# A hybrid encoder layer: small vectors moved ahead of two x tiles, constant rows written by ScalarE, one weight load given its own place

## The reference

```python
h = rms_norm(x, attn_norm)
q, k, v, f_logit, u, cv, cb, cc, g = split(h @ w_in)      # 512,512,512,8,512,512,512,512,3*1024
y_a = forgetting_attention(q, k, v, f_logit, b_f) @ w_proj_attn   # logit bias F[t]-F[s], F = cumsum(log_sigmoid(f))
y_b = multiscale_pool(u, pool_w, pool_scale) @ w_proj_pool        # trailing means of 2/4/8/16 tokens
y_c = short_gated_conv(cv, cb, cc, conv_w) @ w_proj_conv          # B * conv3(C * v)
gates = sigmoid(g + b_gate)
x = x + (gates0 * y_a + gates1 * y_b + gates2 * y_c) @ w_out
a, b = split(rms_norm(x, ffn_norm) @ w_gate_up)           # 2 * 2816
x = x + (silu(a) * b) @ w_down
out = rms_norm(x, final_norm)
```

## Time and profile before

| what | value |
|---|---|
| median of 3 runs | 783.92 us (782.99 to 784.42) |
| profiled execution, its own time | 783.68 us |
| its span (first to last instruction) | 781.2 us |
| TensorE busy | 769.5 us (98%) |
| VectorE busy | 633.4 us (81%) |
| ScalarE busy | 410.1 us (52%) |
| GpSimd busy | 22.8 us (3%), 47 instructions |
| mean granted TensorE clock | 0.998 |
| HBM traffic | 82.87 MB read, 4.19 MB written |

### The profile page before, as it was taken

How to read it: one execution, slowest core, us unless ns; L and a number is a source line. 1 busy time by engine, 2 the same in 40 slices (tenths; PEclk the granted TensorE clock), 3 DMA queues, 4 the chain that set the end, 5 groups by cost and what they waited for, 6 DMA issues and landing times.

```text
span 781.2 us, 12728 instructions
## 1 busy us (share of the span) xinstructions
PE 769.5 (98%) x4491; PEld 682.0 (87%) x4491; DVE 633.4 (81%) x1001; ACT 410.1 (52%) x695; POOL 22.8 (3%) x47
## 2 busy tenths in 40 slices
PE   7999999999999999999999999999999999999996
PEld 5888888888889999999988888999999998888885
DVE  6888686868698878776744599899999986799997
ACT  7265564556445545455434554555555552655554
POOL 5011010100000000000000000000000000000001
PEclk9999999999999999999999999999999999999999
DMA  7433232223243434333363422433333355353422
GB/s 226 118 81 91 69 84 62 77 74 81 81 108 82 108 103 114 93 98 109 108 230 94 152 93 81 122 102 103 109 109 108 110 174 175 117 180 132 149 85 107
DMA packets 130438, 87.81 MB, mean 112 GB/s; under 512 B 5628, under 2 KB 118324, under 8 KB 130388
## 3 DMA queue, kind: packets, MB, share of 16 engines
q1 hardware_dynamic: 129876, 87.08, 37.8%
q0 software_dynamic: 512, 0.07, 0.1%
HBM read 82.87 MB, written 4.19 MB: 111 GB/s over the span
## 4 chain that ended last, share of the span: by engine, by line
PE 96%; DVE 1%; DMA 1%; issue 1%; ACT 0%; POOL 0%; SPq 0%; POOLq 0%; ACTq 0%
PE bank L791 11%; PE bank L795 11%; PE bank L793 11%; PE bank L1170 6%; PE bank L1168 6%; PE bank L1166 6%; PE bank L1222 4%; PE bank L1221 4%; PE bank L981 4%; PE bank L979 4%; PE bank L977 4%; PE bank L1220 4%; PE bank L1015 2%; PE bank L1016 2%; PE bank L1017 2%; PE bank L1059 2%
## 5 line engine op out<-in xcount | busy, mean ns | idle before, releaser
L791 PE MATMUL bank<-operands,whi 128*128 128x512 f32 x384 | 151.6, 395 | 1.3 <-DVE operands L1862 1.3
L795 PE MATMUL bank<-operands,wlo 128*128 128x512 f32 x384 | 149.7, 390 | 0.0
L793 PE MATMUL bank<-operands,whi 128*128 128x512 f32 x384 | 149.6, 389 | 0.0
L1853 DVE TENSOR_TENSOR wlo<-raw,whi 128x1024 fp32r<-128x1024 f32 x55 | 67.1, 1222 | 37.5 <-ACT whi L1286 36.8
L791 PEld LDWEIGHTS bank<-operands,whi 128*128 128x128 f32 x384 | 72.1, 188 | 17.1 <-DVE operands L1862 1.9
L795 PEld LDWEIGHTS bank<-operands,wlo 128*128 128x128 f32 x384 | 72.1, 188 | 15.4
L793 PEld LDWEIGHTS bank<-operands,whi 128*128 128x128 f32 x384 | 72.1, 188 | 14.6 <-issue 0.2
L1286 ACT CAST whi<-raw 128x1024 fp32r<-128x1024 f32 x55 | 57.5, 1049 | 31.1 <-PE bank L1063 21.0
L1166 PE MATMUL bank<-sums_hi,whi 128*128 128x256 f32 x240 | 67.9, 283 | 0.0
L1170 PE MATMUL bank<-sums_hi,wlo 128*128 128x256 f32 x240 | 67.9, 283 | 0.0
L1168 PE MATMUL bank<-sums_lo,whi 128*128 128x256 f32 x240 | 67.9, 283 | 0.0
(11 more groups left out here) (294 smaller groups left out, 1950.7 us busy)
## 6 DMA issues: line engine op xcount, KB each, us to landing
raw<-in_w_in_dram SPq DMA_DIRECT2D x105, 256.0 KB, 3.2
raw<-in_w_gate_up_dram SPq DMA_DIRECT2D x88, 256.0 KB, 3.3
raw<-in_w_down_dram SPq DMA_DIRECT2D x55, 256.0 KB, 2.9
big_x<-in_x_dram SPq DMA_DIRECT2D x8, 512.0 KB, 6.5
raw<-in_w_out_dram SPq DMA_DIRECT2D x16, 256.0 KB, 3.3
raw<-in_w_proj_attn_dram SPq DMA_DIRECT2D x8, 256.0 KB, 4.1
raw<-in_w_proj_pool_dram SPq DMA_DIRECT2D x8, 256.0 KB, 4.0
raw<-in_w_proj_conv_dram SPq DMA_DIRECT2D x8, 256.0 KB, 4.2
```

The costliest lines, as they stand in the source:

```text
L791: nc.tensor.matmul(banks[b][:, 0:width], whi[:, s, w], op(hi + k * S), start=a, stop=False)
L793: nc.tensor.matmul(banks[b][:, 0:width], whi[:, s, w], op(lo + k * S), start=False, stop=False)
L795: mm = nc.tensor.matmul(banks[b][:, 0:width], wlo[:, s, w], op(hi + k * S), start=False, stop=z)
L1853: nc.vector.tensor_tensor(wlo[:, s, :], raw[:, s, :], whi[:, s, :].bitcast(F32), ALU.subtract).then_inc(w_lo, 1)
```

## The change

Three edits, independent of each other.

1. SyncE issues the six small transfers after the second tile of x, and the third and fourth tile after them. The first weights stay where they were, behind all of these.
2. The constant rows: GpSimd adds pairs of neighbouring columns of the identity matrix to get four columns of 128 (`stat` columns 40 to 43), turns two of them negative, and does so before the first `root`. ScalarE then writes each 512-column region as ones times such a column, four activations between `diff_hi(0)` and the cast of the forget columns. The twelve GpSimd instructions are gone.
3. The seventh pair of w_down blocks (`SPARE` = 6) lands in the free columns 7168 to 8191 of `early_32` instead of slot 0 of `raw`, and is issued when `used` reaches NU. The tenth pair (9) then needs slot 0 only to be free of the fourth pair (3).

```diff
-            for t in range(TB):
-                load_x(t)
+            load_x(0)
+            load_x(1)
             for src, at in ((attn_norm, V_ATTN), (ffn_norm, V_FFN), (b_gate, V_GATE),
                             (pool_scale, V_SCALE)):
...
+            for t in range(2, TB):
+                load_x(t)
...
             for r in range(R):
-                sp.wait_ge(w_lo, NU - SLOTS + r + 1 if r < SLOTS else NU + 2 * (r - SLOTS) + 2)
+                if r == SPARE:
+                    sp.wait_ge(used, NU)
+                elif r == SPARE + SLOTS:
+                    sp.wait_ge(w_lo, NU + 2 * (SPARE - SLOTS) + 2)
+                else:
+                    sp.wait_ge(w_lo, NU - SLOTS + r + 1 if r < SLOTS else NU + 2 * (r - SLOTS) + 2)
...
+            pool.wait_ge(consts, 4)
+            for n, (a, row) in enumerate(F_ROWS):
+                r = (1 - a) * HD + row
+                nc.gpsimd.tensor_tensor(stat[:, F_COLS + n:F_COLS + n + 1], ident[:, r:r + 1],
+                                        ident[:, r + 1:r + 2], ALU.add).then_inc(f_consts, 1)
+            pool.wait_ge(f_consts, 4)
+            nc.gpsimd.tensor_scalar(stat[:, F_COLS:F_COLS + 2], stat[:, F_COLS:F_COLS + 2], -1.0,
+                                    None, ALU.mult).then_inc(f_consts, 1)
+
             for t in range(TB):
                 root(t, x1_var, x1_rstd)
 
-            begun = 0
-            for tiles, first, fill in ((Q2, 0, -1.0), (K2, 2, 1.0)):
-                for a in range(2):
-                    rows = op(tiles[a])
-                    nc.gpsimd.memset(rows.bitcast(F32), 0.0).then_inc(f_consts, 1)
...
-            pool.wait_ge(f_consts, F_CONSTS)
+            pool.wait_ge(f_rows, 4)
...
             diff_hi(0)
-            act.wait_ge(f_consts, F_CONSTS)
+            act.wait_ge(f_consts, 5)
+            for n, at in enumerate(Q2 + K2):
+                nc.scalar.activation(op(at), ones[:], ACT.Copy,
+                                     scale=stat[:, F_COLS + n:F_COLS + n + 1]).then_inc(f_rows, 1)
+            act.wait_ge(f_rows, 4)
...
+        def down_raw(k, half, n=1):
+            if k == SPARE:
+                return early_32[:, SPARE_AT + half * HALF:SPARE_AT + (half + n) * HALF]
+            return raw[:, k % SLOTS, half * HALF:(half + n) * HALF]
```

More of the change, by code:

```diff
@@ L398, in hybrid_block @@
         fe = work[0:H, PAD + 3 * S:PAD + 4 * S]
-        F_LOW, F_CONSTS = 32, 12
+        F_LOW, F_COLS, F_ROWS = 32, 40, ((0, 0), (1, 0), (0, 2), (1, 2))
         vec_rows = work[0:N_VECS, PAD + 5 * S:PAD + 5 * S + P]
@@ L415, in hybrid_block @@
         AB, DB_, FB_, EB = (2, 3), (6, 7), (4, 5), (0, 1)
-        N1 = 0
+        SPARE, SPARE_AT = 2 * SLOTS, 2 * DB * S - D
         ROWS4 = [(r,) for r in range(4)] + [(r, r + 1) for r in range(4, R - 1, 2)] + [(R - 1,)]
@@ L445, in hybrid_block @@
         f_in = sem("f_in")
-        f_consts = sem("f_consts")
+        f_consts, f_rows = sem("f_consts"), sem("f_rows")
         final_g_in = sem("final_g_in")
         landed = [sem(f"landed{s}") for s in range(SLOTS)]
+        spare_in = sem("spare_in")
         loads_begun = sem("loads_begun")
@@ L483, in landed_down @@
         def landed_down(k):
+            if k == SPARE:
+                return spare_in, 32
             before = (NU - PARTS + LOADS - PER_TURN * len(TURNS) + TURN_LOADS) // SLOTS * 32
             for q in range(k % SLOTS, k + 1, SLOTS):
-                before += 16 if q == 2 * R else 32
-            return k % SLOTS, before
+                before += {SPARE: 0, 2 * R: 16}.get(q, 32)
+            return landed[k % SLOTS], before
         def wait_full(eng, b, stage, i, k):
@@ L666, in load_down @@
             def load_down(k, blocks):
-                s = k % SLOTS
+                signal = spare_in if k == SPARE else landed[k % SLOTS]
                 for at, (row, c) in enumerate(blocks):
-                    sp.dma_start(raw[:, s, at * HALF:(at + 1) * HALF],
+                    sp.dma_start(down_raw(k, at),
                                  w_down[row * P:(row + 1) * P, c * HALF:(c + 1) * HALF]
-                                 ).then_inc(landed[s], 16)
+                                 ).then_inc(signal, 16)
             for r in range(R):
-                sp.wait_ge(w_lo, NU - SLOTS + r + 1 if r < SLOTS else NU + 2 * (r - SLOTS) + 2)
+                if r == SPARE:
[4 more added lines that the diff above has]
+                    sp.wait_ge(w_lo, NU - SLOTS + r + 1 if r < SLOTS else NU + 2 * (r - SLOTS) + 2)
                 sp.sem_inc(loads_begun, 1)
@@ L1596, in down_hi @@
             def down_hi(r):
-                s, want = landed_down(r)
-                act.wait_ge(landed[s], want)
-                parts_hi(NU + 2 * r, raw[:, s, 0:HALF])
+                act.wait_ge(*landed_down(r))
+                parts_hi(NU + 2 * r, down_raw(r, 0))
                 act.wait_ge(summed, r + 1)
@@ L1783, in _ @@
             for q, rows in enumerate(ROWS3):
-                s, want = landed_down(2 * R + q)
-                act.wait_ge(landed[s], want)
+                s = (2 * R + q) % SLOTS
+                act.wait_ge(*landed_down(2 * R + q))
                 for at, n in in_one(U_3 + rows[0], len(rows)):
@@ L1986, in _ @@
             pool_lo(3, 8)
-            dve.wait_ge(f_consts, F_CONSTS)
+            dve.wait_ge(f_rows, 4)
             for a in range(2):
@@ L2338, in first_sum @@
             def first_sum(r):
-                s, want = landed_down(r)
-                dve.wait_ge(landed[s], want)
+                dve.wait_ge(*landed_down(r))
                 if r == 3:
                     dve.wait_ge(used, NU)
-                nc.vector.tensor_tensor(chain(r), raw[:, s, 0:HALF], raw[:, s, HALF:2 * HALF],
+                nc.vector.tensor_tensor(chain(r), down_raw(r, 0), down_raw(r, 1),
                                         ALU.add).then_inc(summed, 1)
@@ L2604, in second_sums @@
                 k = R + r
-                s, want = landed_down(k)
-                dve.wait_ge(landed[s], want)
+                s = k % SLOTS
+                dve.wait_ge(*landed_down(k))
                 b12, b22 = raw[:, s, 0:HALF], raw[:, s, HALF:2 * HALF]
@@ L2647, in _ @@
             for r in range(3, R):
-                s = r % SLOTS
-                parts_lo(NU + 2 * r, raw[:, s, 0:HALF])
+                parts_lo(NU + 2 * r, down_raw(r, 0))
                 if r + 1 < R:
```

## The result

The changed kernel takes 781.67 us (median of 11 runs, 781.52 to 781.88), the kernel before, run beside it, 783.92 us (11 runs, 782.82 to 784.68). The ratio is 0.9972, 95% interval 0.9964 to 0.998: about 2.2 us faster, 0.28%. Not only the median moved: the runs of the changed kernel lie within 0.4 us of each other, those of the kernel before within 1.9.

The account below looks back on a forecast made before the run. TensorE, busy 98% of the span, was taken to bound the kernel, with waits only at the start. From the median 783.92, -0.8 (constant rows), +0.4 (transfer order) and 0 (seventh pair) gave 783.5 us, range 782.3 to 784.8.

Parts of the forecast that it names:

- the term of +0.4 us for edit 1: Start: third and fourth x tiles, issued behind six small transfers, land later, costing 0.4 us (bounds 0 and +2.6).
- signs of being wrong: Start and after: third x tile used at 10 or later, or 7.3 or sooner, or any TensorE wait after 22 us.
- What bounds the kernel: Whole kernel: TensorE is busy 98% of the span; only its waits at the start, before 22 us, can be won.
- Edit 2, the term of -0.8 us inside the span: Start: without GpSimd's rows VectorE's half tiles and first split shorten by 0.27, 0.27, 0.42, together 0.96; 0.8 us reaches TensorE.
- Edit 2, what it adds: Start: five small GpSimd instructions (at most 2.75 us) and four ScalarE activations (2.4 us) hide in idle time, cost 0.
- Rival 2: Start: small transfers delay the third x tile now; moved, it lands at 7.0, total 782.0 us; chance 0.09.
- Rivals 1 and 4: Start: late issue, or small transfers holding queues one by one, delays x by 2.6 us, total 785.7; chances 0.03 and 0.02.
- rival 3: Start: GpSimd's work was not what held VectorE, so the total is 784.3 us, same as before; chance 0.10.
- Edit 3: Stage down: removes VectorE's 0.92 us wait for a w_down pair, but TensorE does not wait there; value 0.

Follow-up runs that it names:

- `l_rows_later`: Kernel before with GpSimd's twelve constant-row instructions kept but moved behind VectorE's split of the first weights; 783.31 us, ratio 0.9996.
- `g_spaced`: Kernel before, small transfers still behind all of x, but SyncE waits for the first tile's landing before issuing the third and fourth; 783.05 us, ratio 0.9992.
- the first four experiments: Kernel before with only the transfer order, constant rows or seventh pair changed, or the first two together; 782.95, 782.45, 783.63, 781.77 us.

## Why the prediction was wrong

The step that failed is the term of +0.4 us for edit 1: the third tile was to be used 0.4 us later than in the profile before, and it was used earlier, at 6.98 us. That is one of the signs of being wrong that the prediction names (7.3 or sooner). A second term, the time outside the span, was missing. Term by term:

- **What bounds the kernel** was right: after 22 us no kernel of this study but `l_rows_later` gave TensorE an idle time, and all of the gain within the span is at the start.
- **Edit 2, the term of -0.8 us inside the span**, was right in mechanism and size. VectorE's half tiles and first split got 0.24, 0.24 and 0.42 us shorter, 0.90 against the 0.96 of the sum; 0.73 reached TensorE at equal landing. In the changed profile it is ScalarE's first high part that is late next, as the sum said, though it costs 0.34 instead of about 0.1, and the landing of the weights' second half stands ahead of it.
- **Edit 2, what it adds**: nothing on the path. The five GpSimd instructions took 0.96 us together, not the bound of 2.75; the four activations 2.55 (2.4 forecast) under a cover of 2.76.
- **Edit 2, outside the span**: 0.5 us that the sum did not have. It took the 2.5 us around the span as fixed. This term alone moves the forecast from 783.5 to 783.0, still inside the range.
- **Edit 1, the term of +0.4 us, failed in its sign.** "The third tile's data could then begin at 5.05 to 5.55 [...] I take +0.4": the tile was used at 6.98 to 7.33 when issued about 2 us later. (It was issued at 3.75, not 4.3: the six issues took 2.09 us, and the 0.82 of the last one that the 2.6 contains is 0.30 here.) The step read the landing of one profiled execution, 8.07 and 9.49, as what the queues take, while it is one draw of a landing that varies from 7.3 to 8.3; the runs' spread of 1.4 us, which the text took only as the limit of what can be told apart, was a sign of it. Edit 1 is worth 0.5 us by the median (783.46 to 782.95, interval of the ratio just including 1), 0.7 on top of edit 2 (782.45 to 781.77), and 0.1 to 0.3 by the shortest run. What moved the landing inside the queues stays open.
- **Rival 2** came nearest to the outcome, with 782.0 us and a third tile at 7.0, at a chance of 0.09. That hit is luck: its cause is not borne out. The small transfers need not leave the third tile's way, since in `g_spaced` they are issued behind all of x, from 4.80, and the tile is used at 7.12; and with x and the transfers issued as before it was used at 7.29 and 7.32 as well. Rivals 1 and 4 (the transfers' issue or their number holds x back by 2.6 us) are out, with the tile used at 7.33 or sooner behind all six; so is rival 3 (GpSimd not at fault), by edit 2 alone.
- **Edit 3** is worth 0, as forecast.

With measured terms, on the medians of the first four experiments: 783.46, less 1.0 for edit 2 (0.7 in the stream and 0.5 outside the span, by profiles), less 0.7 for edit 1 on top of it, gives 781.8, against 781.77 for the two together. Beside the changed kernel itself the median before was 783.92 and the gain 2.25: how many long runs fell among the eleven before may be part of that.

## What to carry to other kernels

Where a start waits for tiles in flight, one profile's landing times are one draw: look at the spread of the runs and at their granted clock first, and try the same transfers issued in two groups. Work of GpSimd's that nobody waits for soon can still cost time, if it stands beside VectorE's path (0.90 us of VectorE here); move it to another engine with idle time, as here to ScalarE, or beside VectorE's operations with one SBUF and one PSUM input. When a wait is cleared from a start, ask which engine still has idle time there: the next 0.6 us here came from giving GpSimd work back, at a place where it does no harm.

## What the runs showed of the hardware

- A GpSimd memset of 512 columns holds off VectorE's multiply of an SBUF tile by a column (0.48 us alone, 0.72 beside it), not its two-input subtraction (0.67 beside a memset, 1.10 beside a select). VectorE's low parts with one input in PSUM are not touched by either, nor by a GpSimd subtraction (0.67 to 0.69 per block of a row in all).
- GpSimd's subtraction of 128x512 float32 columns takes 1.28 us, VectorE's 0.68.
- With four 512 KB loads issued within 1.8 us the third was used at 7.29 to 8.27 us (five profiles); with the third issued about 2 us later, at 6.98 to 7.33 (six profiles). The bytes and the order of x are the same.
- Runs of the kernel before at a mean granted clock of 0.994 to 0.996 took 783.72 to 785.27 us (16), those at 0.997 or more 782.82 to 783.97 (45).
- The part of the execution outside the span depends on GpSimd's instructions: 2.46 us with 47 of them, 1.96 with 40, 2.11 with twelve small memsets more, 2.19 with the selects turned into memsets (the last two in single runs).
